# Scaling attention probabilities inside the TensorE turn, by a diagonal of reciprocals

## The reference

```python
h = h + even_mixer(rms_norm(h), w_in, w_out)      # layer 0: 8 softmax heads + 4 retention heads
h = h + hier_moe(rms_norm(h), ...)                # top-1 of 4 groups, top-2 of 8 experts in it
h = h + odd_mixer(rms_norm(h), w_in, w_out)       # layer 1: 16 softmax heads (dilated windows)
h = h + hier_moe(rms_norm(h), ...)
return rms_norm(h)
...
s = q @ k.T * scale + mask                        # per head, 256 queries, head size 64
p = softmax(s)                                    # exp(s - max) / sum
o = p @ v
```

## Time and profile before

| | |
|---|---|
| median of three runs | 1159.32 us (1158.4 to 1159.6) |
| the profiled execution, its own time | 1156.15 us |
| its span, first to last instruction | 1154.3 us |
| busy share of the span | PE 75%, DVE 34%, ACT 21%, POOL 3% |
| DMA | 441.22 MB, mean 382 GB/s |
| mean granted clock of TensorE | 0.892 of full speed |

### The profile page before, as it was taken

How to read it: one execution, slowest core, us unless ns; L and a number is a source line. 1 busy time by engine, 2 the same in 40 slices (tenths; PEclk the granted TensorE clock), 3 DMA queues, 4 the chain that set the end, 5 groups by cost and what they waited for, 6 DMA issues and landing times.

```text
span 1154.3 us, 21809 instructions
## 1 busy us (share of the span) xinstructions
PE 864.9 (75%) x9162; PEld 548.8 (48%) x9162; DVE 393.1 (34%) x990; ACT 238.5 (21%) x618; POOL 29.1 (3%) x47
## 2 busy tenths in 40 slices
PE   8997979966665757576799888799566666666774
PEld 6875745534342424243478667355243434343432
DVE  6886633322121212121278654233121212121212
ACT  5554401110000001000165752111000000000002
POOL 0002000000000000000000220000000000000000
PEclk9998989988787888788999999899887879797888
DMA  9878399999999999999996565999999999999995
GB/s 347 269 305 334 144 403 425 426 430 428 428 429 429 428 429 428 429 428 429 410 387 254 229 257 218 380 426 427 429 429 428 428 429 429 428 430 428 428 426 223
DMA packets 54270, 441.22 MB, mean 382 GB/s; under 512 B 11856, under 2 KB 12368, under 8 KB 29648
## 3 DMA queue, kind: packets, MB, share of 16 engines
q1 hardware_dynamic: 54080, 440.07, 91.9%
q10 hardware_dynamic: 144, 0.52, 0.1%
HBM read 439.53 MB, written 1.05 MB: 382 GB/s over the span
## 4 chain that ended last, share of the span: by engine, by line
PE 42%; DMA 38%; DVE 6%; SPq 5%; ACT 4%; another core or an unknown queue 3%; issue 2%; POOL 0%; POOLq 0%; ACTq 0%; DVEq 0%
DMA ring<-in_w_expert_up 21%; DMA ring<-in_w_expert_down 17%; PE bank L985 13%; PE bank L1004 5%; PE bank L883 3%; PE bank L885 3%; PE bank L884 3%; PE bank L967 3%; PE bank L1017 3%; SPq L436 2%; SPq L440 2%; PE bank L1053 1%; PE bank L1055 1%; PE bank L1054 1%
## 5 line engine op out<-in xcount | busy, mean ns | idle before, releaser
L985 PE MATMUL bank<-ring,scratch 128*32 128x256 f32 x4096 | 302.0, 460 | 178.7 <-DMA ring<-in_w_expert_up 177.2
L985 PEld LDWEIGHTS bank<-ring,scratch 128*32 128x32 f32 x4096 | 156.5, 131 | 319.3 <-issue 207.9
L1440 DVE TENSOR_SCALAR scratch<-scratch 128x128 f32<-128x128 f32 x64 | 14.5, 227 | 634.5 <-ACT scratch L686 612.7
L685 ACT ACTIVATE scratch<-bank 128x128 f32<-128x128 f32 x64 | 17.8, 278 | 601.7 <-PE bank L985 583.0
L1004 PE MATMUL bank<-ring,h 128*32 128x256 f32 x2048 | 127.2, 389 | 12.9 <-DMA ring<-in_w_expert_down 12.8
L1017 PE MATMUL bank<-h 32*128 32x256 f32 x1024 | 74.3, 402 | 37.2 <-ACT h L693 37.2
L1004 PEld LDWEIGHTS bank<-ring,h 128*32 128x32 f32 x2048 | 63.9, 111 | 57.1 <-issue 25.6
L1017 PEld LDWEIGHTS bank<-h 32*128 32x128 f32 x1024 | 50.0, 186 | 66.8 <-issue 66.7
L883 PE MATMUL bank<-split,h_high 128*128 128x512 f32 x192 | 77.7, 404 | 3.6 <-DVE split L1240 3.6
L1240 DVE SCALAR_TENSOR_TENSOR split<-ring,gains,split 128x512 fp32r<-128x512 f32 x96 | 68.2, 749 | 27.4 <-ACT split L728 26.7
L885 PE MATMUL bank<-split,h_high 128*128 128x512 f32 x192 | 75.0, 391 | 0.0
(11 more groups left out here) (179 smaller groups left out, 742.4 us busy)
## 6 DMA issues: line engine op xcount, KB each, us to landing
ring<-in_w_expert_gate SPq DMA_DIRECT2D x64, 2048.0 KB, 47.3
ring<-in_w_expert_up SPq DMA_DIRECT2D x64, 2048.0 KB, 48.9
ring<-in_w_expert_down SPq DMA_DIRECT2D x64, 2048.0 KB, 48.6
ring<-in_w_in_even SPq DMA_DIRECT2D x5, 2048.0 KB, 17.5
ring<-in_w_in_odd SPq DMA_DIRECT2D x5, 2048.0 KB, 19.8
ring<-in_w_out_even SPq DMA_DIRECT2D x2, 2048.0 KB, 9.7
ring<-in_w_out_odd SPq DMA_DIRECT2D x2, 2048.0 KB, 11.5
h<-in_x SPq DMA_DIRECT2D x2, 512.0 KB, 4.4
```

Of the source, the lines that this page charges most:

```text
L985: last = pe.matmul(psum[6][32 * j:32 * j + 32, 0:2 * P].rearrange("p (a s) -> p a s", a=2), xT[:, c, SLOTS * k:SLOTS * k + SLOTS], ring[:, ...
```

## The change

- PE's `turn_p` is now a true matmul of the probabilities with a diagonal matrix that holds the reciprocals of the row sums (`inv_sum`), in place of a transpose with the identity. DVE's `head_sum` builds this diagonal: one reciprocal, and behind it two multiplications of the 128x128 identity by it. POOL's multiplication of the probabilities is gone.
- Scores of items 0 and 1 are issued inside the last projection block (after its chunk 3), and the first four output weight chunks are split there too, on ACT and on DVE, in place of after the block.
- Layer 0 scores are issued one head at a time; layer 1 still goes by pairs. In layer 1 ACT takes the exponentials of heads 0 and 1 ahead of the copies of the last block.
- `low_oT` of pair a moves from step 2a + 7 to 2a + 8, where that is not beyond the last head.
- The diagonals lie in unit 6, so the SP queue loads the fourth expert's pair after all heads are turned, in place of after all scores.
- The two halves of the output are stored in the other order.

```diff
-        rden = small[:, 40:88].rearrange("p (h b) -> p h b", b=3)
+        rden = small[:, 40:72].rearrange("p (h t) -> p h t", t=T)
+        inv_sum = ring[:, KT_AT, 2048:3072].rearrange("p (i t s) -> p i t s", i=4, t=T)
...
-                sp.wait_ge(s_done[l], n_items[l])
+                sp.wait_ge(p_turned[l], HEADS[l])
...
-            for t in range(T):
+            for t in reversed(range(T)):
                 sp.wait_ge(out_ready[t], 1)
...
-                for m in range(HEADS[l]):
-                    if l == 0 and m == 3:
-                        pool.wait_ge(ret_var, 1)
-                        pool.tensor_tensor(rrstd, rvar, half_exp[:, 0:1].broadcast_to([P, 8]),
-                                           ALU.pow).then_inc(ret_pow, 1)
-
-                    pool.wait_ge(den_ready[l], m + 1)
-                    b = prob[(n_ret[l] + m) % 4].rearrange("p (b s) -> p b s", b=3)
-                    pool.tensor_tensor(b, b, rden[:, m, :].unsqueeze(2).broadcast_to([P, 3, P]), ALU.mult)\
-                        .then_inc(p_ready[l], 1)
+                if l == 0:
+                    pool.wait_ge(ret_var, 1)
+                    pool.tensor_tensor(rrstd, rvar, half_exp[:, 0:1].broadcast_to([P, 8]), ALU.pow).then_inc(ret_pow, 1)
...
-                    if j == NW:
+                    if l and j == NW:
+                        for m in range(2):
+                            exponentials(l, m)
+                    if j > ROTATED[l]:
+                        block_out(l, j - 1)
+                    if j == NW - 1:
                         for at in MIX_TURNS[:MIX_BEGUN]:
                             split_mix(l, *at)
-                    if j > ROTATED[l]:
-                        block_out(l, j - 1)
...
             def retention_scores(n):
-                if n:
-                    pe.wait_ge(ret_ready, n)
...
+                if n >= 2:
+                    pe.wait_ge(ret_ready, n - 1)
...
             def scores(l, m):
-                held = m if l == 0 else m - 2
-                if held > 0:
-                    pe.wait_ge(s_out[l], held)
+                if m >= 2:
+                    pe.wait_ge(s_out[l], m - 1 if l == 0 else m - 2)
                 elif l == 0:
-                    pe.wait_ge(ret_ready, RET)
+                    pe.wait_ge(ret_ready, RET - 1 + m)
...
             def turn_p(l, m):
...
-                    last = pe.transpose(psum[2 + m % 2][:, P * b:P * b + P], b4[:, P * b:P * b + P], ident)
+                    last = pe.matmul(psum[2 + m % 2][:, P * b:P * b + P], b4[:, P * b:P * b + P],
+                                     inv_sum[:, m % 4, min(b, 1), :], start=True, stop=True)
...
                     project(l, j, 0, TURN_AT[0])
+                    if j == NW - 1:
+                        pe.wait_ge(qkT_ready[l], n_rot[l])
+                        for b in range(2):
+                            pe.wait_ge(bank_out[l][b], 3)
+                        for i in range(2):
+                            item_scores(l, i)
...
             def head_sum(l, m, link):
                 dve.wait_ge(exp_done[l], m + 1)
-                dve.reciprocal(rden[:, m, 0:2], den[:, m, :])
-                dve.reciprocal(rden[:, m, 2:3], den[:, m, 1:2]).then_inc(den_ready[l], 1)
+                if m >= 4:
+                    dve.wait_ge(p_turned[l], m - 3)
+                link(dve.reciprocal(rden[:, m, :], den[:, m, :]))
+                for t in range(T):
+                    last = dve.tensor_scalar(inv_sum[:, m % 4, t, :], ident, rden[:, m, t:t + 1], None, ALU.mult)
+                last.then_inc(p_ready[l], 1)
...
-                    else:
+                    if j == NW - 1:
                         for at in MIX_TURNS[:MIX_BEGUN]:
                             low_mix(*at)
...
+                low_pair = {2 * a + LAG + (5 if 2 * a + LAG + 5 <= HEADS[l] else 4): a for a in range(HEADS[l] // 2)}
...
-                    a, odd = divmod(m - LAG - 4, 2)
-                    if a >= 0 and not odd:
-                        low_oT(a)
+                    if m in low_pair:
+                        low_oT(low_pair[m])
```

More of the change, by code:

```diff
@@ L357, in build @@
         exp_done = sems("exp_done", LAYERS)
-        den_ready = sems("den_ready", LAYERS)
         p_ready = sems("p_ready", LAYERS)
@@ L779, in _ @@
                 for i in range(HEADS[l] + LAG + 4):
-                    if i < HEADS[l]:
+                    if (2 if l else 0) <= i < HEADS[l]:
                         exponentials(l, i)
@@ L899, in retention_scores @@
             def retention_scores(n):
-                if n:
-                    pe.wait_ge(ret_ready, n)
[L903 to L910, removed]
+                if n >= 2:
+                    pe.wait_ge(ret_ready, n - 1)
+                bank, rows = psum[n % 2], slice(HEAD * (n % 2), HEAD * (n % 2) + HEAD)
+                q, k = qT[rows, 4 + n // 2, :], kT[rows, 4 + n // 2, :]
+                pe.matmul(bank[:, 0:2 * P], k[:, 0:P], q, start=True, stop=True, tile_position=(rows.start, 0))
+                pe.matmul(bank[:, 2 * P:3 * P], k[:, P:SEQ], q[:, P:SEQ], start=True, stop=True,
+                          tile_position=(rows.start, 0)).then_inc(s_done[0], 1)
             def scores(l, m):
-                held = m if l == 0 else m - 2
-                if held > 0:
-                    pe.wait_ge(s_out[l], held)
+                if m >= 2:
+                    pe.wait_ge(s_out[l], m - 1 if l == 0 else m - 2)
                 elif l == 0:
-                    pe.wait_ge(ret_ready, RET)
-                heads = [(score_bank(l, m + b), slice(HEAD * b, HEAD * b + HEAD)) for b in range(2)]
+                    pe.wait_ge(ret_ready, RET - 1 + m)
+                heads = [(score_bank(l, n), slice(HEAD * (n % 2), HEAD * (n % 2) + HEAD))
+                         for n in ((m,) if l == 0 else (m, m + 1))]
                 q, k = qT[:, m // 2, :], kT[:, m // 2, :]
@@ L926, in scores, with item_scores @@
                               tile_position=(rows.start, 0)).then_inc(s_done[l], 1)
+            def item_scores(l, i):
+                if i < n_ret[l]:
+                    retention_scores(i)
+                elif l == 0 or i % 2 == 0:
+                    scores(l, i - n_ret[l])
             def retain(n):
@@ L1115, in _ @@
                     project(l, j, TURN_AT[1], C)
-                pe.wait_ge(qkT_ready[l], n_rot[l])
-                for b in range(2):
-                    pe.wait_ge(bank_out[l][b], 3)
                 for i in range(n_items[l] + LAG + 3):
                     m = i - n_ret[l]
[L1121 to L1124, removed]
+                    if 2 <= i < n_items[l]:
+                        item_scores(l, i)
                     if i == 2:
@@ L1530, in _ @@
                         copy_pT(l, m - LAG)
-                    a, odd = divmod(m - LAG - 4, 2)
-                    if a >= 0 and not odd:
-                        low_oT(a)
+                    if m in low_pair:
+                        low_oT(low_pair[m])
                     if l == 0 and m == HEADS[l] + 3:
+                        dve.wait_ge(retT_high, T)
                         for t in range(T):
-                            dve.wait_ge(retT_high, t + 1)
                             dve.tensor_tensor(o_low[:, 0:4, P * t:P * t + P],
```

## The result

Twenty executions of each kernel gave medians of 1157.19 us before and 1160.76 us after: a ratio of 1.0032, with a 95% interval of 1.0022 to 1.0041. The changed kernel is slower by 2.5 to 4.7 us, just over the 0.2% that the prediction took as what can be told from no change. The forecast time is met (1160.8), but not the difference: +1.5 was forecast and +3.6 came. The three executions shown of before had a median of 1159.32, 2.1 us above its later one, and that fills the gap.

The account below looks back on a forecast made before the run. Experts run at DMA speed, so only how early each mixer ends was taken to move the end. Layer 0 +4.0, layer 1 -2.1, stores -0.4 gave +1.5; 1159.3 + 1.5 = 1160.8 us, range 1157.5 to 1165.0.

Parts of the forecast that it names:

- What bounds the kernel: Experts run at DMA speed; a microsecond won or lost in a mixer, up to its first expert, reaches the end one for one.
- The last block of layer 0: Layer 0's last projection block: splits put ahead delay DVE by 1.0 and PE further, so head 0's maximum starts 1.4 us later.
- the early scores win nothing: Layer 0: early scores of items 0 and 1 win nothing, because DVE has no time for them.
- The heads of layer 0: Layer 0's heads on DVE: eight dearer sums +4.2, POOL's lock gone -1.2, fewer waits -0.7 us.
- the lock: Layer 0: two DVE multiplications held up by POOL's operations, 0.75 each against 0.17, are freed: -1.2 us.
- last turn: Layer 0's last head, ahead of the output product: turning by three true matmuls takes 0.77 against 0.48, +0.3 us.
- Layer 1: Layer 1's heads: later `low_oT` cuts the DVE-ACT loop, turn 14 2.7 us earlier; two dearer turns +0.6; together -2.1.
- The fourth pair's load: The fourth expert's load waits some 7 us longer for the turns, while the DMA stands idle: cost 0.
- stores: End of the program: half 1 is ready before half 0, so the other store order gives -0.4 us.
- The diagonals are dear: Rival: diagonals on DVE cost 0.34 each in both layers' heads; total +5.5, 1164.8 us, slower; chance 0.28.
- The clock falls earlier in layer 0: Rival: PE's clock falls in the middle of layer 0's heads, about +2; total +3.5, 1162.8 us; chance 0.12.
- The clock does not fall: Rival: PE's clock stays up in layer 0, total -1.1, chance 0.05; also in layer 1's gather (1.6), -2.7, chance 0.10.

Follow-up runs that it names:

- the new order in layer 1 alone: Layer 0 as before; layer 1 in the changed order but with the old transposes and Pool scaling: 1148.40 us, ratio 0.9930 to the kernel before.
- the turn by transposes: Changed kernel, diagonals still made but turns by the old transposes, probabilities unscaled; only head stages compared: layer 1's pair of heads takes 3.08 us.
- the one without diagonals: Changed kernel, true matmuls against the identity, no diagonals made; only head stages compared: layer 1's pair of heads takes 3.38 us.
- early splits alone: Kernel before with layer 0's first four output chunks split ahead of the last projection block, and the new store order: 1161.36 us, ratio 1.0029.
- The single-items run: Kernel before with layer 0's scores one item at a time, items 0 and 1 ahead of the block's end, new store order: 1157.80 us, ratio 1.0002.
- late splits: Changed kernel with layer 0's first four output chunks split after the last projection block, as before: 1157.48 us, ratio 1.0002 to the kernel before.
- order alone: Changed kernel with the transposes and the Pool engine's scaling put back in both layers: 1152.43 us, ratio 0.9964 to the kernel before.

## Why the prediction was right, and where it was not

**The time** came out to 0.1 us, and that is luck: the difference was +3.6 where +1.5 was forecast, and the median that the forecast started from lay 2.1 too high. The direction was right. The likeliest case of the prediction was a difference within 0.2% (0.50); what came, 0.32% slower, was its case of 0.40. Both layers came out worse than forecast, layer 0 by 1.4 and layer 1 by 0.8 in the pair of profiles.

**What bounds the kernel** held up to the mixers' ends. The mixers' ends come out at the end of the program; with the new order in layer 1 alone, the last addition stands 7.8 us earlier (147.20 + 549.85 = 697.05) and the profiled execution is 8.2 shorter (1147.99), 0.4 of it the stores. It held less well for the stretch from there to the refill: layer 1's refill came another 1.6 earlier in the changed kernel, and the experts behind it at most 0.7. The DMA is at work there already (0.99 to 1.01 of its share from 714.53 to 724.53), on down weights that SP issues at the last addition.

**The last block of layer 0 (forecast +1.4, measured +2.6 net)** is the step that failed. DVE's part was right (+1.0). What was too small is the rest, PE's way from there to head 0's maximum: the router weights start at 84.25 and the maximum 7.22 later, while before it was 5.59. With the splits back in their place it is 5.78, although the scores are single there too. So it takes PE's late end of the block for the queue of `retain` and single scores to cost anything. Of the missing 1.2, the clock's fall at 80 is 0.4: in the two kernels of the changed order in which it stayed up there, the turn by transposes and the one without diagonals, the distance is 6.82 and 6.86. Most of the rest lies behind the block. The prediction has its end at 85.9 and the maximum at 89.6, 3.7 later; measured are 4.40 in the changed kernel and in the one with transposes, since a `retain` of 0.86 and a score of 0.86 stand between item 3's turn on DVE and head 0's (89.75 and 91.47, 1.7 apart, where 1.3 was put down). The sentence that the early scores win nothing does not hold either: the run with early splits alone, which lacks them and the single items, needs 5.58 there.

**The heads of layer 0 (forecast +4.2 - 1.2 - 0.7 = +2.3, measured +2.9).** `head_sum` is 0.60 where 0.65 was forecast, and the lock went as forecast. What is left over, 1.0, must be waits, those for single scores among them; this is by subtraction, and no run has them apart. The Pool engine's power, which might have held up a diagonal, did not: it runs from 100.12 for 1.64, and the two diagonals at 100.75 took their usual 0.48. The **last turn** and the way into the output product were put at +0.3; the product starts at 110.60, 6.13 late, so 5.5 net, and of these 2.6 + 2.9 are the two steps above. The sum for layer 0, +4.0, measures +5.4 at the refill. The way from first tile to first refill is 5.33 in both profiles.

**Layer 1 (forecast -2.1, measured -1.3 in the pair of profiles).** The loop through DVE and ACT was read rightly: cutting it alone wins 7.1 us. But the term that takes its place was mis-sized, and with it the engine that sets the pace. DVE at 3.2 was put as the pace and PE at 3.1; measured are 3.08 for DVE and 3.39 for PE. A turn of three true matmuls costs 0.86, not 0.77, and a pair's scores 0.86, not 0.76. Head 14's turn starts 4.0 late (679.69) in a layer that starts 5.7 late (the loads ahead of it at 594.49 and 588.80): -1.7, where -2.7 was forecast, and six pairs by the 0.2 between 3.2 and 3.39 are about that missing 1.0. The last column of the table moves by more than this at equal code; the pair's 3.39 does not, it stands in all four profiles with this layer 1 or its matmuls.

**The fourth pair's load** was issued 10.4 later in layer 0 (114.49 against 104.12; some 7 was forecast) and shows no cost: the down weights behind it are issued 5.66 later (122.80 against 117.14), as late as the mixer. No run tests it alone. The **stores** gave the 0.4.

**The rivals.** *The diagonals are dear* is out: 0.20 each. *The clock falls earlier in layer 0* comes nearest by its time (+3.5 for +3.6), but not by its place: in the changed kernel the clock fell in the projection, for 0.4, and stayed up through the heads. The single-items run shows what that rival would have looked like. *The clock does not fall* did not occur in layer 0 of the changed kernel: it fell from 110 to 114, in the output product, as before did from 103 to 110. Its second half did occur: layer 1's gather ran at 1.00, the refill came the forecast 1.6 earlier, and of that at most 0.7 reached the experts behind it.

**What stays open** is how much of each median is the clock's doing. Six profiles with the old layer 0 (one with a later low part) put its first tile at 148.90, 146.87, 147.20, 148.28, 147.70 and 148.18. The kernel before was profiled at the late end of these, so its one profile makes layer 0's loss look about 1 us too small. Nor do the times and the profiles agree on layer 0's heads: with late splits the rest of the change in layer 0 costs 1.4 us by the ratios (1.0002 against 0.9990, intervals that overlap), while the diagonals alone are 3.2 in the heads. And single items cost nothing in the times and early splits alone 3.4, though the two profiles look alike (155.07 and 154.38); here the profile of the single items is of an execution 6.8 above the median of its kind, that of the early splits of one 0.6 above.

## What to carry to other kernels

When two engines wait for each other around a loop, look for the one instruction that stands a step too early in a queue: here one `low_oT`, one head later, won 7 us (5.2 in its profile) and was worth more than all else of the change. Before you take work from an idle engine (here the Pool engine, 0.83 us a head, for which PE had no wait once the loop was cut), count what its replacement costs on the engines that will set the pace once the loop is cut. And judge a change with several parts in several stages part by part: +3.7 in all was -8.1 for the best of its parts.

## What the runs showed of the hardware

In four profiles of the same order of work the clock goes with the kind of turn. From 98 to 108 us, PE with transposes (order alone) ran at a granted clock of 0.52, and with matmuls (changed) at 1.00, though it was busy for less of the time:

```profile
98.00:108.00 10.00, 9.50 (x36) 5.67 (x38) 9.34 (x46) 6.53 (x26) 5.71 (x6) 0.52 0.63 265
```

```profile
98.00:108.00 10.00, 7.64 (x52) 5.43 (x52) 9.58 (x53) 6.28 (x25) 1.64 (x1) 1.00 0.58 245
```

The run with transposes and diagonals (clock 0.50 from 100 to 108) and the one with matmuls and no diagonals (1.00 from 70 to 130) say the same. The Trainium skill, *TensorE: Matmul & The Clock Gate*, Part 4, says of transposes that they do not count as PE activity in the same way, and these four agree. Others speak against a simple rule: with matmuls and late splits the clock was at 0.50 from 100 to 108 too, and with transposes and early splits alone it was at 1.00 there until 106. So it is not shown that the kind of turn decides. And the higher clock bought nothing in these heads, where DVE was the one to wait for: 18.61 with it, 18.62 without.

The same code does not get the same clock each time: in the kernel before it fell near 103, in the two kernels with the old layer 0 and a new layer 1 between 92 and 96. In the last projection block with early splits, PE's wait of 1.94 to 1.95 was followed by a clock of 0.50 in two of the four profiles of the changed order, and not in the other two.

A transpose of three float32 pieces passes PE in 0.48 us and the same three as true matmuls in 0.86, a factor of 1.8, both at a granted clock of 1.00. A multiplication of a 128x128 float32 tile by a value per row follows another on DVE after 0.20.
